# The residual additions at the end of both feed-forwards: every second one moved from VectorE to GpSimd

## The reference, cut to what matters

```python
def rms_norm(x, g):
    xf = x.astype(jnp.float32)
    y = xf * lax.rsqrt(jnp.mean(xf * xf, axis=-1, keepdims=True) + EPS)
    return (y * g.astype(jnp.float32)).astype(x.dtype)
...
        fx = conv_ffn(modulate(rms_norm(x, g_pre_ffn[l]), mx[3], mx[4]), w_up[l], w_conv[l], b_conv[l], w_down[l])
        x = x + mx[5] * rms_norm(fx, g_post_ffn[l])
```

## Time and profile before

| | us |
|---|---|
| median of three runs | 3430.04 (3428.70 to 3430.66) |
| the profiled execution | 3429.06 |
| its span, first to last instruction | 3427.2 |
| TensorE matmul busy | 3187.3 (93%) |
| VectorE (DVE) busy | 2154.7 (63%) |
| ScalarE (ACT) busy | 1324.0 (39%) |
| GpSimd (POOL) busy | 1126.6 (33%) |

### The profile page before, as it was taken

How to read it: one execution, slowest core, us unless ns; L and a number is a source line. 1 busy time by engine, 2 the same in 40 slices (tenths; PEclk the granted TensorE clock), 3 DMA queues, 4 the chain that set the end, 5 groups by cost and what they waited for, 6 DMA issues and landing times. The chain is left out here.

```text
span 3427.2 us, 49511 instructions
## 1 busy us (share of the span) xinstructions
PE 3187.3 (93%) x18000; PEld 2563.6 (75%) x18000; DVE 2154.7 (63%) x3314; ACT 1324.0 (39%) x2061; POOL 1126.6 (33%) x1155
## 2 busy tenths in 40 slices
PE   6989899998999999999998889899998699999996
PEld 4876577776788888888886676677776578888885
DVE  4754588875544444444446764578875667777777
ACT  3431466664421121111112441476663333333332
POOL 1323455552110000000001332355551455556653
PEclk9989999999999999999999899999999899999998
DMA  6557300104321111111105466201013211111112
GB/s 241 193 187 271 139 23 33 35 20 157 111 68 37 37 37 37 37 37 37 39 28 188 151 216 248 107 33 35 32 66 127 71 53 55 49 49 52 55 52 117
DMA packets 189956, 304.91 MB, mean 89 GB/s; under 512 B 13446, under 2 KB 139918, under 8 KB 178534
## 3 DMA queue, kind: packets, MB, share of 16 engines
q1 hardware_dynamic: 187685, 302.04, 25.6%
q10 hardware_dynamic: 2113, 0.77, 0.1%
HBM read 234.58 MB, written 68.19 MB: 88 GB/s over the span
## 5 line engine op out<-in xcount | busy, mean ns | idle before, releaser
L132 PE MATMUL banks<-h_hT,up_u_hi 128*128 128x512 f32 (+1 forms) x1056 | 375.2, 355 | 7.2 <-DVE up_u_lo L1990 5.7
L133 PE MATMUL banks<-h_hT,up_u_lo 128*128 128x512 f32 (+1 forms) x1056 | 374.7, 355 | 0.0
L134 PE MATMUL banks<-h_hT,up_u_hi 128*128 128x512 f32 (+1 forms) x1056 | 374.4, 355 | 0.0
L132 PE MATMUL banks<-ff_d_lo,ff_a_hi 128*128 128x512 f32 x792 | 316.2, 399 | 25.4 <-DVE h_acc L3159 12.5
L134 PE MATMUL banks<-ff_d_hi,ff_a_hi 128*128 128x512 f32 x792 | 309.1, 390 | 0.0
L133 PE MATMUL banks<-ff_d_hi,ff_a_lo 128*128 128x512 f32 x792 | 309.0, 390 | 0.0
L2424 POOL TENSOR_TENSOR ff_ms<-ff_ss,c_eps 128x1 f32<-128x1 f32 x10 | 10.1, 1009 | 898.7 <-ACT ff_t_gate L2535 898.7
L2575 DVE TENSOR_TENSOR ff_acc<-banks,ff_acc 128x512 f32<-128x512 f32 x220 | 150.7, 688 | 175.2 <-PE banks L134 175.0
L1558 PE MATMUL banks<-c_ident,al_prA 128*128 128x128 f32 x1312 | 214.9, 278 | 20.0 <-ACT al_oTC L1861 18.6
L3159 DVE TENSOR_TENSOR h_acc<-banks,h_acc 128x512 f32<-128x512 f32 x336 | 224.9, 689 | 4.1 <-PE banks L134 0.9
L132 PEld LDWEIGHTS banks<-h_hT,up_u_hi 128*128 128x128 f32 x1056 | 200.2, 190 | 36.1 <-issue 5.9
(11 more groups left out here) (351 smaller groups left out, 8128.7 us busy)
## 6 DMA issues: line engine op xcount, KB each, us to landing
kv_m_wm<-in_w_mod_dram SPq DMA_DIRECT2D x40, 1024.0 KB, 5.1
up_u_raw<-in_w_up_dram SPq DMA_DIRECT2D x44, 512.0 KB, 3.9
ff_d_raw<-in_w_down_dram SPq DMA_DIRECT2D x44, 512.0 KB, 3.3
hT_d<-fr_hs SPq DMA_DIRECT2D x20, 1024.0 KB, 5.3
st_hs<-hT_d SPq DMA_DIRECT2D x20, 1024.0 KB, 6.9
q_d<-fr_qs SPq DMA_DIRECT2D x18, 512.0 KB, 3.1
q_d<-fr_qs SPq DMA_DIRECT2D x36, 256.0 KB, 3.0
al_quA<-q_d SPq DMA_DIRECT2D x18, 512.0 KB, 4.0
```

What stands on the lines that cost most here:

```text
L132: e.matmul(out, w[0], x[1], start=start, stop=False)
L133: e.matmul(out, w[1], x[0], start=False, stop=False)
L134: return e.matmul(out, w[0], x[0], start=False, stop=stop)
```

## The change

The scaling stays on VectorE. The addition of the residual goes to GpSimd for tiles 0, 2, 4 and 6 of ten in the first layer and for tiles 0, 2 and 4 of eight in the second. On GpSimd it stands behind the two small steps for tile t+2. SP waits for the one or the other engine's semaphore, tile by tile, in the same order as before.

```diff
@@ ffn_phase
+        added_pool, BY_POOL = ph.sem("added_pool"), range(0, n - 2, 2)
@@ SP queue
-                e.wait_ge(added, t + 1)
+                if t in BY_POOL:
+                    e.wait_ge(added_pool, t // 2 + 1)
+                else:
+                    e.wait_ge(added, t + 1 - len([m for m in BY_POOL if m < t]))
@@ GpSimd, after the two small steps of tile t
+                if t - 2 in BY_POOL:
+                    e.wait_ge(scaled, t - 1)
+                    e.wait_ge(x_in[t % 2], 16 * ((t - 2) // 2 + 1))
+                    e.tensor_tensor(acc[:, t - 2, :], acc[:, t - 2, :], x[t % 2], ALU.add).then_inc(added_pool, 1)
@@ VectorE, residual(t), between the scaling and the addition
+                if t in BY_POOL:
+                    return
```

More of the change, by code:

```diff
@@ L2802, in ffn_halves_phase @@
         sq_done, pow_done, scaled, added, stored = (ph.sem(m) for m in ("sq_done", "pow_done", "scaled", "added", "stored"))
+        added_pool, BY_POOL = ph.sem("added_pool"), range(0, N - 2, 2)
         up_done = hv.up_done
@@ L2897, in _ @@
                 e.tensor_tensor(rs[:, t:t + 1], ms[:, t:t + 1], c.minus_half[:, 0:1], ALU.pow).then_inc(pow_done, 1)
+                if t - 2 in BY_POOL:
+                    e.wait_ge(scaled, t - 1)
+                    e.wait_ge(x_in[t - 2], 16)
+                    e.tensor_tensor(acc[:, t - 2, :], acc[:, t - 2, :], x[t - 2][:, :], ALU.add).then_inc(added_pool, 1)
         @block.tensor
```

## The result

The changed kernel takes 3433.88 us (median of 20 runs, 3431.40 to 3437.84), the kernel before 3429.97 (20 runs, 3426.57 to 3433.06): ratio 1.0015, 95% interval 1.0009 to 1.0021. It is slower by 3.9 us. The interval leaves out 1, so the kernel is slower, by about 3 to 7 us; the 3.9 us are within 0.2%. The forecast was +3.1 and "same". The two medians shown ahead of the prediction and here (3430.04 and 3429.97) are of the same kernel, with 3 and with 20 runs.

A forecast was written before the change was run, and what follows sets the result against it. The second layer's end was taken as bound by VectorE, the first's as beginning so and ending bound by DMA. +0.5 and +2.6 gave +3.1 us: 3432.2 profiled, 3433.1 for the median; range 3430.0 to 3437.5.

The forecast's parts named there:

- same: Whole kernel: time within about 0.2%, 6.9 us, of the kernel before, which measurement cannot tell from no change.
- the row that I chose: Profile row of a GpSimd subtraction of two 128 x 1024 SBUF tiles, 2.39 us, taken as the moved addition's cost.
- Rival A: Both layers: the two engines do overlap; second layer gains 3.4 us, first layer 0, time 3426.6; chance 0.06.
- +2.6 forecast: Second layer: first moved addition costs 1.1 us, the two others 0.76 each; bounds 2.0 and 3.2.
- 0.76: Cost in us of one steady moved addition, the odd tile's scaling waiting for GpSimd's addition to end.
- S + 5.67: End of the odd tile's scaling with the change, S being the even tile's scaling start; before, S + 4.91.
- 1.14 are saved, 1.90 are waited: Per moved addition, VectorE saves its addition but waits for GpSimd's, costing about 0.76 us.
- not 1.1: Second layer, first tile: VectorE's own addition ends at 3404.2 instead of 3403.13, costing 1.1 us.
- +0.5 forecast: First layer: last addition ends at 1889.1 instead of 1888.6, set by late residual loads; bounds 0 and +4.2.
- the line has become short: at the 4.1 us of an unhindered load: First layer: residual load 8, issued 2.7 us late, takes 4.1 us and lands at 1885.4 instead of 1884.4.
- Rival B: First-layer loads decide, load 6 again taking 8.6 us; with 3.2 in the second layer +7.4, 3437.4; chance 0.07.
- its 4.2: First layer's upper bound in us, where every delay of the residual loads goes through.

The follow-up runs named there:

- the memset run: Against the kernel before: second-layer residual additions of tiles 0, 2, 4 left out, GpSimd writing zeros of similar length instead; stretch 21.93 us, ratio 0.9992.
- the run without the additions: Against the kernel before: second-layer residual additions of tiles 0, 2, 4 left out on both engines; stretch 21.91 us, ratio 0.9989.
- the other loads moved away: Change in first layer only, on the kernel before with three weight loads and two next-layer tile loads issued after tile 7; stretch 39.21 us, ratio 1.0007.

## Why the prediction was right

**The mechanism.** That operations on two SBUF tiles take turns between the two engines carried the sign, and it stands: the pieces end one behind the other, the memset run points to the reading as the cause, and the scalings of tiles 3 and 5 took 3.21 and 3.16 us (forecast 3.3). The GpSimd addition takes 2.39 us, as the row that I chose; the estimate from the Trainium skill's figure (GPSIMD Engine Reference, section Performance versus the Vector engine) was 2.25. Rival A is out; its gain would have been 3.8 us and not 3.4, as the run without the additions shows.

**The second layer, +2.6 forecast, +2.06 measured.** Both terms were somewhat too large. A steady moved addition cost 0.65, not 0.76. The 0.76 was taken between ends (S + 5.67 against S + 4.91), and these were off by a few hundredths each: GpSimd's addition ended at S + 4.51 and not 4.54, the scaling 1.09 after it and not 1.13, and before it had ended at S + 4.93. The gloss beside it, "1.14 are saved, 1.90 are waited", does not fit the same steps, which give 1.24 and 2.00; both terms were 0.1 too small, so the difference held. (The 1.14 did mislead the expectation for the run without the additions, 22.3 us against 21.91.) The first tile cost 0.76 and not 1.1: I had VectorE's scaling wait for GpSimd's one-column power, but the scaling was issued at 3402.18, in the midst of that power (3401.98 to 3402.53), and took its plain 1.28. That is 0.2 of the 0.3; the rest is that GpSimd's addition ended 2.20 us after the scaling and not 2.3.

**The first layer, +0.5 forecast, +1.36 measured (1.80 with that layer alone).** The step that failed is "the line has become short: at the 4.1 us of an unhindered load": the loads of tiles 8 and 9 took 5.9 and 6.1 us. The DMA view of the changed kernel, for the loads issued at 1872.67, 1881.27 and 1883.61:

```profile
ff_x<-xs_d SPq DMA_DIRECT2D x1, 512.0 KB, 5.7
...
ff_x<-xs_d SPq DMA_DIRECT2D x1, 512.0 KB, 5.9
...
ff_t_value<-xs_d SPq DMA_DIRECT2D x1, 512.0 KB, 6.1
```

Tile 6's load was issued 3.3 us later against the first scaling (20.87 us on instead of 17.54) and took 5.7 us instead of 8.6, so that most of the delay did vanish in the backlog, as forecast: it landed 0.4 us late (forecast 0.9). Tile 8's load then went out only 1.6 us late and not 2.7, because GpSimd added tile 6 at once, ahead of VectorE's scaling of tile 7, where I had the scaling go first. These 1.1 us too much hid a good part of the 1.8 us by which the load's time was too short: tile 8 landed 1.7 us late (forecast 1.0) and tile 9 2.5 us behind it, as forecast. That the end was only 0.9 us off is partly luck.

What TensorE does in the pauses that VectorE's waits make was in none of my steps. Tiles 4 and 5 cost 1.2 us and not 0.76, in waits for matmuls at half clock, while GpSimd's addition (1869.86 to 1872.26) was wholly covered. But the chain that set the end did not run through it: tile 6's addition on GpSimd did not follow the power at once but 0.14 us after its end, when its load had landed, and that load had gone out as soon as GpSimd had added tile 4, 4.52 us after the start of tile 4's scaling, exactly as for tile 2 at full clock. With the first layer alone the profile names this wait. GpSimd's timeline with the change in both layers, and in the first alone:

```profile
1877.86 0.54 POOL L2430 TENSOR_TENSOR ff_rs<-ff_ms,c_minus_half 128x1 f32<-128x1 f32 x1
1878.54 2.34 POOL L2434 TENSOR_TENSOR ff_acc<-ff_acc,ff_x 128x1024 f32<-128x1024 f32 x1
```

```profile
1880.88 2.35 POOL L2434 TENSOR_TENSOR ff_acc<-ff_acc,ff_x 128x1024 f32<-128x1024 f32 x1 [0.32 <-DMA ff_x<-xs_d]
```

So three of the signs that I had named for the first layer did not come: the scaling of tile 5 was not lengthened (1.27 us, while those of tiles 1 and 3 took 2.32 and 2.33), GpSimd waited 0.1 to 0.3 us for load 6 and not long in VectorE's stead, and landings 8 and 9 were late by 1.7 and 1.4 us, not by 1 or less. Rival B is out as priced: the loads did not let every delay through, and load 6 took 5.7 us. That the cost rose to 3.98, near its 4.2, with the other loads moved away does not bear it out: there load 6 took 4.0 us, and 2.5 of the 3.98 stood before tile 6 was scaled.

**The sum** +3.1 against +3.4 in the two stretches and +3.9 in the medians: the errors of the two layers, 0.5 too much and 0.9 too little, partly cancelled, which is luck.

## What to carry to other kernels

Before work is moved from VectorE to GpSimd, ask what VectorE will be doing during it: under accumulates from PSUM the piece is free, under operations on two SBUF tiles it is paid in full, at GpSimd's slower rate and with everything that stands behind it on GpSimd's queue. What counts is the whole of GpSimd's work in the window, the small steps too, and a wait of this kind does not show as idle time but as a longer instruction. Where the stretch is bound by loads as well, part of the cost is hidden, and the cheaper gain may lie in the order of the DMA issues: moving three weight loads took 2.65 us off the same stretch of the kernel before. Such gains need not add to the change, though: with the change in place, moving them and two more loads took nothing off.

## What was not expected of the hardware

- Two pauses of TensorE of 2.25 to 2.3 us, 8 us apart, were followed by a fall of the granted clock to 0.50 in all three runs that have the change in the first layer, and by matmuls of 0.63 us instead of 0.40; pauses of 0.65 us in the kernel before were not. That the pauses are the cause is argued from their order, not tried by itself.
- A one-column GpSimd power that had already started did not lengthen a two-tile VectorE operation issued 0.20 us after it (1.28 us), and the same in the runs with the additions left out and with the memset; whereas small steps issued under a running two-tile VectorE operation waited in these stretches (1.2 and 1.5 us instead of 0.19 and 0.55).
- The 512 KB loads share the DMA engines with what is issued after them: a residual tile's load took 4.0 to 4.6 us with little else under way, 4.7 to 5.3 when it was issued 2.3 to 2.9 us behind another, and up to 8.6 with several loads issued close before or behind.
